# Alternating the units of v and of the output gate, with longer stretches of substitution between v's convolutions

## What is computed

```python
p = h @ w_in
qkv = jax.nn.silu(dwconv3(p[..., :QKV_END], conv_qkv))
gate = p[..., QKV_END:GATE_END]
m = jnp.where(strict, jnp.einsum("bhncd,bhnsd->bhncs", kb, k) * decay, 0.0)
u = lax.linalg.triangular_solve(m + eye, vb, lower=True, unit_diagonal=True)
w = lax.linalg.triangular_solve(m + eye, kb * jnp.exp(gc)[..., None], ...)
# scan over the chunks with u, w, q, k and the state, forward and backward
o = rmsnorm(o_f + flip(o_b), o_norm_g) * jax.nn.silu(gate)
y = jnp.concatenate([o_a, y_b], axis=-1) @ w_out
```

## Time and profile before

| what | us |
|---|---|
| median of 3 runs | 1558.63 |
| the runs | 1558.63, 1550.22, 1558.81 |
| the profiled execution, its own time | 1558.17 |
| its span, first to last instruction | 1556.4 |
| PE busy in the span | 1416.7 |
| DVE busy in the span | 991.7 |
| mean granted TensorE clock | 0.967 of full speed |

### The profile page before, as it was taken

One profiled execution on the slowest core, in us unless ns is written; L12 is line 12 of the kernel. 1 busy time (PEld: TensorE's weight loads), 2 busy tenths in 40 slices (PEclk: granted clock), 3 DMA queues, 4 the chain that ended last, 5 costly groups with the idle time before them and its releaser, 6 DMA issues.

```text
span 1556.4 us, 24698 instructions
## 1 busy us (share of the span) xinstructions
PE 1416.7 (91%) x9517; PEld 1374.8 (88%) x9517; DVE 991.7 (64%) x1377; ACT 410.1 (26%) x719; POOL 659.3 (42%) x400
## 2 busy tenths in 40 slices
PE   2799999869969799999999999986999999999995
PEld 1598879769969699999999999975999999999995
DVE  4785698967676567688878788445654155425554
ACT  4623322137250533301110111156331011001122
POOL 0253464300504255556447555311454545454542
PEclk9799999889989899999999999998999999999998
DMA  9232212242223223543334433210332222222122
GB/s 377 102 108 96 95 41 69 86 171 97 91 71 106 70 95 129 184 164 124 130 118 170 136 122 112 76 41 14 117 112 79 70 81 67 71 78 81 66 71 79
DMA packets 44646, 162.18 MB, mean 104 GB/s; under 512 B 4784, under 2 KB 5936, under 8 KB 43568
## 3 DMA queue, kind: packets, MB, share of 16 engines
q1 hardware_dynamic: 44592, 161.47, 30.1%
HBM read 153.07 MB, written 5.77 MB: 102 GB/s over the span
## 4 chain that ended last, share of the span: by engine, by line
PE 78%; DVE 10%; ACT 4%; issue 3%; DMA 2%; POOL 1%; SPq 0%; ACTq 0%; DVEq 0%; POOLq 0%
PE ps L662 68%; PE ps L946 1%; PE ps L674 1%; ACT work L1015 1%; DVE work L1452 1%; DVE qkv L1554 1%; DMA x<-in_x 1%; DVE junk L1435 1%; DVE blocks L1628 1%; PE ps L821 1%; DVE ada_raw L1435 1%; PE ps L823 1%; PE ps L900 1%; PE ps L898 1%; PE ps L888 1%
## 5 line engine op out<-in xcount | busy, mean ns | idle before, releaser
L587 POOL TENSOR_SCALAR whi<-raw 128x1024 fp32r<-128x1024 f32 (+1 forms) x172 | 192.3, 1118 | 754.7 <-PE ps L662 566.0
L662 PE MATMUL ps<-hhi,whi 128*128 128x320 f32 x1984 | 460.1, 313 | 41.0 <-DVE hlo L1419 31.5
L662 PE MATMUL ps<-hlo,whi 128*128 128x320 f32 x1984 | 455.1, 311 | 0.0
L662 PE MATMUL ps<-hhi,wlo 128*128 128x320 f32 x1984 | 454.9, 310 | 0.0
L590 POOL TENSOR_TENSOR wlo<-raw,whi 128x1024 fp32r<-128x1024 f32 (+1 forms) x172 | 433.0, 2518 | 14.3
L662 PEld LDWEIGHTS ps<-hhi,whi 128*128 128x128 f32 x1984 | 335.0, 190 | 49.6 <-issue 28.6
L662 PEld LDWEIGHTS ps<-hlo,whi 128*128 128x128 f32 x1984 | 335.5, 190 | 0.0
L662 PEld LDWEIGHTS ps<-hhi,wlo 128*128 128x128 f32 x1984 | 335.0, 190 | 0.0
L662 PE MATMUL ps<-hidhi,whi 128*128 128x320 f32 x704 | 160.5, 309 | 4.5 <-POOL wlo L590 3.0
L662 PE MATMUL ps<-hidhi,wlo 128*128 128x320 f32 x704 | 160.2, 308 | 0.0
L662 PE MATMUL ps<-hidlo,whi 128*128 128x320 f32 x704 | 160.1, 308 | 0.0
(11 more groups left out here) (204 smaller groups left out, 1308.8 us busy)
## 6 DMA issues: line engine op xcount, KB each, us to landing
raw<-in_w_gu SPq DMA_DIRECT2D x88, 512.0 KB, 3.2
ada_raw<-in_w_rows SPq DMA_DIRECT2D x70, 512.0 KB, 3.5
raw<-in_w_in SPq DMA_DIRECT2D x28, 512.0 KB, 3.3
raw<-in_w_dn SPq DMA_DIRECT2D x32, 448.0 KB, 3.3
ada_first<-in_w_ada SPq DMA_DIRECT2D x4, 2048.0 KB, 22.8
raw<-in_w_dn SPq DMA_DIRECT2D x16, 512.0 KB, 3.4
row_late<-in_w_rows SPq DMA_DIRECT2D x10, 512.0 KB, 3.2
raw<-in_w_out SPq DMA_DIRECT2D x8, 512.0 KB, 4.3
```

Source lines behind the costliest of these rows:

```text
L587: nc.gpsimd.tensor_scalar(whi[s][:, 0:n], raw[s][:, 0:n], 1.0, 0.0, ALU.mult, ALU.add).then_inc(s_whi, 1)
L662: last = nc.tensor.matmul(pair[pr][:, b], wt[s][:, cs], act[:, k, b * HALF:(b + 1) * HALF], start=(j == 0 and q == 0), stop=(j == len(tile ...
```

## The change

The gate's units go between those of v: units 20 to 27 become v0, g0, v1, g1, v2, g2, v3, g3. All four of v now use pair A and all four of the gate pair B. The weights are reordered on the host. ScalarE does `taken(v_j)` and `gate(j)` in turn, and both expansions after the last gate. VectorE's second pass keeps its 30 steps and its three convolutions, but cuts the steps 9, 10 and 11 long around them instead of 3, 4 and 23. SyncE's and POOL's programs are not edited.

```diff
-U_B, U_V, U_G = NQK, NQK + 3 * NB, NQKV + 3 * NB
+U_B, U_V = NQK, NQK + 3 * NB
-                nc.scalar.activation(halves(pad[s]), pair["AB"[s]], ACT.Copy).then_inc(s_ev["AB"[s]], 1)
+                nc.scalar.activation(halves(pad[s]), pair["AB"[u % 2]], ACT.Copy).then_inc(s_ev["AB"[u % 2]], 1)
-            for j in range(NQKV - NQK):
-                taken(U_V + j, j % 2, NQK + NB + j, NQK + j)
             def gate(j):
-                u = U_G + j
+                u = U_V + 2 * j + 1
-            gate(0)
+            for j in range(NGATE):
+                taken(U_V + 2 * j, j % 2, NQK + NB + j, NQK + j)
+                gate(j)
             expand_pair(0)
-            gate(1)
             expand_pair(1)
-            gate(2)
-            gate(3)
             def value_conv(j):
-                u, s = U_V + j, j % 2
-                dve.wait_ge(s_ev["AB"[s]], PRIMED + u // 2 + 1)
+                u, s = U_V + 2 * j, j % 2
+                dve.wait_ge(s_ev["A"], PRIMED + u // 2 + 1)
             lanes_in(NT)
-            substitute(1, 4)
+            substitute(1, 10)
             value_conv(2)
-            substitute(4, 8)
+            substitute(10, 20)
             value_conv(3)
-            substitute(8, BLOCK - 1)
+            substitute(20, BLOCK - 1)
-IN_ORDER = [..., *range(NQK, NQKV + NGATE)]
+IN_ORDER = [..., *(j + e for j in range(NQK, NQKV) for e in (0, NGATE))]
```

More of the change, by code:

```diff
@@ L1873, in _ @@
                     nc.vector.tensor_tensor(yout[:, k, :], yout[:, k, :], rstd, ALU.mult).then_inc(s_ychunk[0], 1)
-IN_ORDER = [*range(NQK), *(NQKV + NGATE + p * NB + j for j in range(NB) for p in (1, 2, 0)), *range(NQK, NQKV + NGATE)]
+IN_ORDER = [*range(NQK), *(NQKV + NGATE + p * NB + j for j in range(NB) for p in (1, 2, 0)), *(j + e for j in range(NQK, NQKV) for e in (0, NGATE))]
 def kernel(**inputs):
```

## The result

The changed kernel takes 1569.32 us (median of 6 runs, 1564.16 to 1574.08); before takes 1557.8 us (6 runs, 1550.22 to 1558.81). The ratio is 1.0076 with a 95% interval of 1.0056 to 1.0096: slower by some 12 us, and within 1%. The profiled execution took 1572.07 us, its span is 1570.3, 13.9 us longer than before's.

The account below looks back on a forecast made before the run. The path from v3's silu through zeros and expansions to SyncE's moves was to decide, hiding PE's 8.0 us gain: 10.75 at SyncE plus 2.45 in transfer on 1558.17 gave 1571.4, put at 1571.5 us, range 1563 to 1577.

Parts of the forecast that it names:

- a path that would be 13.2 us later: v3's silu, zeros, two expansions, ys6, SyncE's moves, then cond_late landing: 10.75 us at SyncE plus 2.45 in transfer.
- PE's side: Units 20 to 27: gap closed, unit 27 ends at 318.8, 8.0 us earlier, worth nothing behind SyncE's wait.
- the two short gaps: PE's waits before units 25 and 27, 0.8 and 1.5 us, costed at no clock loss.
- VectorE's side: Second pass: no work added, but v3's convolution ends at 321.75, 15.9 us later.
- POOL's split at 295.88: Collision of POOL's weight split with VectorE's second pass, forecast at about 295.8 and costed at 2.8 us.
- SyncE's side: Queue after v3's silu: zeros, expansions, ys6, loads; first move at 337.6 instead of 326.85, 10.75 us later.
- The transfer term: ys6 and output weights in flight with the moves delay cond_late further: +2.45 us, 15.6 us of engine work.
- the sum: Whole kernel: -8.0 on PE worth nothing, +10.75 at SyncE, +2.45 in transfer; 1571.4 us for the profiled execution.
- All else in the merge follows from it: Merge after cond_late: shifts with cond_late's landing at +13.2 us, no further term.
- the clock at the merge is as low as before: PE's clock at the merge: unchanged, since PE idles in both kernels.
- its forecast: Whole kernel: the case of +10.75 to +15.1 us, 1569 to 1573.5 us, chance 0.60.

Follow-up runs that it names:

- f_mid_moves: Changed kernel with SyncE's moves ahead of the wait for the expansions and VectorE's stretches cut to 3, 7 and 20 steps; 1545.9 us, ratio to before 0.9927.
- d_late_ys6: Changed kernel with ys6's zeroing and two weight loads issued behind cond_late, the wait for the expansions still ahead of the moves; 1565.12 us, ratio to before 1.0055.
- a_order_only: Changed kernel with VectorE's old stretches (3, 4 and 23 steps), keeping the alternated units; 1562.67 us, ratio to before 1.0034.
- g_before_moves: Kernel before with only SyncE's queue reordered: moves and cond_late ahead of the wait for the expansions, ys6 and weight loads; 1556.84 us, ratio to before 0.9994.
- b_stretches_only: Kernel before, old unit order kept, with the new VectorE stretches of 9, 10 and 11 steps; 1571.24 us, ratio to before 1.0098.
- c_moves_first: Changed kernel with SyncE's moves and cond_late issued ahead of the wait for the expansions, ys6 and two weight loads; 1554.22 us, ratio to before 0.9981.

## Why the prediction was right

It forecast 1571.5 us and no gain, from a path that would be 13.2 us later; the medians differ by 11.5 us, the spans of the profiled executions by 13.9. Point by point:

- **PE's side.** Unit 27 was forecast at 311.7 to 318.8, and the trace has it at 311.71 to 318.99; the two short gaps (0.64 and 1.05 us) cost no clock, as was assumed. f_mid_moves, where the moves follow unit 27, shows that this gain is real and was only hidden.
- **VectorE's side.** v3's convolution was put at 321.75, by the start of the product behind it, which is at 321.23 in the trace. The argument, that work on a queue without waits is conserved, so that the convolution ends when only steps 20 to 30 are left, held to 0.5 us. The difference is where POOL's split at 295.88 fell. It began beside VectorE's transpose, which took 2.05 us instead of 1.93, and then held up one addition for 2.29 us instead of 0.21: 2.2 us in all, where I had kept 2.8. The rule of the Trainium skill's page "SBUF — State Buffer" had given 0.4 us less than 2.8; the trace agrees with it in kind, and the saving was 0.6.
- **SyncE's side.** The first move was put at 337.6 and came at 336.20, 9.35 us later than before instead of 10.75. Of the 1.4 us, 0.5 are VectorE's and 0.9 are the zeroing's: 7.6 us from its issue to the first expansion, not the 8.5 of the trace of before. In the eight traces this takes 7.6 to 8.7 us; why it varies is open.
- **The transfer term was too large.** I took 2.45 us for the backlog of `ys6` and the output weights; it was 14.48 - 13.11 = 1.37 us, and d_late_ys6, without that backlog, has 13.15. That the engines would be full was right: their share from the first move until `cond_late` was there was 1.01. What was too large is their work, 15.6 us in the sum against 1.01 x 14.4 = 14.5 here. The row:

```profile
336.20:350.60 14.40, 1.62 (x8) 1.22 (x7) 2.59 (x2) 0.00 (x0) 0.00 (x0) 0.50 1.01 366
```

  By the last column 366 x 14.4 is 5.3 MB, and the rows that the sum was made from the earlier trace rows give 309 x 4.9 + 323 x 12.7 = 5.6 MB, at 2.8 us of engine time per MB in both. So some 0.3 MB less went ahead of `cond_late` than in before. Which transfer that was is not shown; the two row tiles issued behind `cond_late` are candidates.
- **A term was missing.** "All else in the merge follows from it" and "the clock at the merge is as low as before" are not quite so. The first pair of the merge runs at the lower clock in both kernels, but for longer in the changed one: the first 16 matmuls of L821 and 16 of L823 take 359.92 - 353.21 = 6.7 us, before 347.74 - 342.49 = 5.25. That is 1.5 us. The windows show it: before, the clock rises 2 to 4 us into the merge, after, it is still low at 6.

```profile
344.50:346.50 2.00, 2.00 (x16) 2.00 (x15) 0.45 (x1) 1.50 (x5) 0.00 (x0) 0.76 0.00 0
```

```profile
357.20:359.20 2.00, 2.00 (x12) 2.00 (x11) 0.58 (x1) 0.00 (x0) 0.00 (x0) 0.50 0.00 0
```

  The first row is of before, the second of the changed kernel. PE's longer wait ahead of the merge (15.4 us, before 12.4) does not explain it by itself: in a_order_only PE waits 14.9 us, and the same 32 matmuls take 5.6; in d_late_ys6 it waits 12.7 us and they take 6.3; in g_before_moves 11.9 and 5.6. Whether the change has a part in it stays open.
- **The last 1.7 us** of the span's difference are the clock behind POOL's split, above, and no part of the prediction.

So the number is in part luck. The path moved by 10.7 us where the sum has 13.2: 1.4 us less up to the first move, 1.1 less in the transfers. The merge added 1.5 us that the sum did not have, and the clock far behind it 1.7 more in the profiled execution. The medians differ by 11.5 us, and 1569.32 lies at the lower end of what the prediction calls its forecast, 1569 to 1573.5. What was right without luck is the mechanism: which path decides, and that PE's gain is hidden behind it.

## What to carry to other kernels

A gap of the busiest engine is worth closing only if the engine's end is what comes last at the next meeting point; look there first, and note how much the other paths have to spare (here 4.45 us, used up more than three times over by moving one convolution 15 us back). In a queue in program order each wait also holds what stands behind it, so an order that costs nothing today can become the bound once the work in front is rearranged; edit the queue together with the schedule. When work is cut into stretches around an item that others wait for, put the item where its input arrives, not later.

## What the runs showed of the hardware beyond that

The same program text up to the change starts v0's silu at 275.4 to 280.4 us in eight profiled executions (two kernels show 279.4, others 275.38, 275.52, 277.21, 277.29, 277.44, 280.39). So up to 5 us of an execution's time are set in the first 80 us, by nothing that was edited: the first of the eight copies at L1022 starts at 60.9 to 65.4 us already. Between 40 and 60 us the granted clock was 0.75 in the execution that came last of these to v0's silu and 0.91 in the one that came first:

```profile
40.00:60.00 20.00, 19.33 (x119) 12.63 (x117) 11.81 (x10) 11.01 (x16) 0.69 (x1) 0.75 0.01 4
```

```profile
40.00:60.00 20.00, 14.80 (x116) 10.14 (x116) 15.96 (x15) 11.95 (x18) 5.00 (x3) 0.91 0.01 5
```

The first is g_before_moves, the second f_mid_moves. PE was busy 19.33 and 14.80 us there with nearly the same number of matmuls. It is this spread that makes a difference of 5 us hard to see in single runs, and it is why the distances above are counted from v0's silu.

A second such place is PE's wait for POOL's split, some 820 us into the execution, 3.0 to 3.3 us long in all eight. From the first load of ScalarE's table at L995 to the second it takes 487.0 to 487.4 us in before, b_stretches_only, c_moves_first and f_mid_moves, 488.9 in the changed kernel, and 489.7 to 489.8 in a_order_only, d_late_ys6 and g_before_moves. In g_before_moves, which has the units and stretches of before, the clock behind that wait is 0.66 over 10 us, with 41 matmuls where before has 59. The length of the wait does not decide it: 3.0 us cost the clock in a_order_only, and 3.3 us did not in b_stretches_only. So one execution can be 2.8 us longer than another by this alone, in either unit order.
